# A hybrid FNet, retention and expert step: the Fourier branch over mirrored halves of channels and positions

## The reference

```python
h = _rmsnorm(x, norm1_g) * (1.0 + sc1) + sh1          # sc1, sh1, g1, ...: columns of silu(cond) @ w_ada
proj = h @ w_in                                       # 5120 columns: u_f 1024, q k v g 512 each, gate_f gate_r 1024 each
uf = u_f.reshape(b, length, 8, 128)
f_mix = jnp.fft.fftn(uf, axes=(1, 3), norm='ortho').real   # over positions and over the 128 channels of a group
f_out = f_mix.reshape(b, length, 1024) @ w_four
...                                                   # retention over q, k, v in both directions, group norm, silu(g)
merged = sigmoid(gate_f) * f_out + sigmoid(gate_r) * r_out
x = x + g1 * (merged @ w_o)
```

## Time and profile before

| | |
|---|---|
| Median of three runs | 971.39 us |
| Lowest and highest | 969.62 and 971.8 us |
| The profiled execution | 971.8 us |
| Its span, first to last instruction | 969.9 us |
| TensorE busy | 926.9 us, 96% |
| TensorE weight loads | 429.8 us, 44% |
| VectorE busy | 501.1 us, 52% |
| ScalarE busy | 211.4 us, 22% |
| Mean granted TensorE clock | 0.99 of full speed |

### The profile page before, as it was taken

The page is one execution under the profiler, slowest core; times in us unless marked ns, Lnnn a source line. Parts: engine busy times, 40 slices in busy tenths (PEclk is TensorE's granted clock), DMA queues, the critical chain, the costliest instruction groups (busy, mean ns, idle before and its releaser), DMA issues.

```text
span 969.9 us, 11638 instructions
## 1 busy us (share of the span) xinstructions
PE 926.9 (96%) x4219; PEld 429.8 (44%) x4251; DVE 501.1 (52%) x1045; ACT 211.4 (22%) x405; POOL 52.1 (5%) x68
## 2 busy tenths in 40 slices
PE   3999999999999999999999999999999999999992
PEld 2446444855555545853343333333333434333330
DVE  3102520695678673564454545454545454545457
ACT  4111201210000012512222222222222222222222
POOL 1010000100000000010000000000000000000000
PEclk9999999999999999999999999999999999999996
DMA  9993222304547646618999999999999999999901
GB/s 332 391 331 144 88 86 87 120 1 173 217 173 261 238 189 268 239 44 360 422 420 422 419 422 417 422 419 419 418 417 414 420 421 418 419 413 419 409 29 66
DMA packets 63995, 285.82 MB, mean 295 GB/s; under 512 B 6345, under 2 KB 6529, under 8 KB 38721
## 3 DMA queue, kind: packets, MB, share of 16 engines
q1 hardware_dynamic: 57216, 265.56, 68.6%
q0 software_dynamic: 6720, 19.50, 5.3%
HBM read 286.24 MB, written 3.80 MB: 299 GB/s over the span
## 4 chain that ended last, share of the span: by engine, by line
PE 92%; DMA 3%; DVE 2%; ACT 1%; issue 1%; SPq 0%; DVEq 0%; POOLq 0%; ACTq 0%
PE bank L1086 22%; PE bank L697 15%; PE bank L1119 13%; PE bank L1112 11%; PE bank L690 11%; PE bank L879 4%; DMA ring<-in_w_in 2%; PE bank L1022 2%; PE bank L920 2%; PE bank L713 2%; PE bank L1025 1%; PE bank L927 1%; PE bank L1097 1%; DMA VG<-h_rows,idx 1%; PE bank L965 1%; PE bank L745 1%
## 5 line engine op out<-in xcount | busy, mean ns | idle before, releaser
L1086 PE MATMUL bank<-ring,QK 128*64 128x512 f32 (+1 forms) x1184 | 225.3, 592 | 0.0
L1086 PEld LDWEIGHTS bank<-ring,QK 128*64 128x64 f32 (+1 forms) x1184 | 72.3, 130 | 147.7 <-issue 147.7
L1119 PE MATMUL bank<-Fm,VG 128*128 128x512 bf16 x544 | 124.5, 383 | 6.5 <-DVE Fm L1990 3.0
L1975 DVE TENSOR_TENSOR hT<-bank,hT 128x512 f32<-128x512 f32 x192 | 118.3, 683 | 5.3 <-PE bank L1119 4.2
L1112 PE MATMUL bank<-ring,VG 128*64 128x512 f32 (+1 forms) x592 | 116.9, 598 | 0.5 <-ACT VG L1433 0.5
L690 PE MATMUL bank<-ring,hT 128*128 128x512 f32 x240 | 103.8, 593 | 0.0
L1966 DVE SCALAR_TENSOR_TENSOR VG<-VG,cw,bank 128x256 f32<-128x256 f32 x32 | 15.4, 481 | 144.5 <-issue 138.1
L1984 DVE TENSOR_TENSOR Fm<-bank,Fm 128x512 f32<-128x512 f32 x64 | 44.3, 692 | 83.2 <-ACT Fm L1440 83.2
L1119 PEld LDWEIGHTS bank<-Fm,VG 128*128 128x128 bf16 x576 | 56.5, 99 | 67.9 <-DVE Fm L1990 3.7
L697 PE MATMUL bank<-hT,ring 128*128 128x384 f32 x256 | 85.4, 487 | 0.0
L1440 ACT CAST Fm<-bank 128x512 bf16<-128x512 f32 x64 | 37.5, 586 | 207.3 <-PE bank L1112 207.3
(11 more groups left out here) (367 smaller groups left out, 810.8 us busy)
## 6 DMA issues: line engine op xcount, KB each, us to landing
ring<-in_w_exp_gate SPq DMA_DIRECT2D x64, 1024.0 KB, 10.9
ring<-in_w_exp_up SPq DMA_DIRECT2D x64, 1024.0 KB, 13.2
ring<-in_w_exp_down SPq DMA_DIRECT2D x64, 1024.0 KB, 13.0
ring<-in_w_ada SPq DMA_DIRECT2D x12, 2048.0 KB, 10.8
ring<-in_w_in SPq DMA_DIRECT2D x10, 2048.0 KB, 16.9
ring<-in_w_four_out SPq DMA_DIRECT2D x2, 2048.0 KB, 7.7
ring<-in_w_out SPq DMA_DIRECT2D x2, 2048.0 KB, 11.2
ring<-in_w_ret_out SPq DMA_DIRECT2D x1, 2048.0 KB, 14.1
```

What stands on the lines that cost most here:

```text
L1086: ins = mm(ps[0][rows, :], xT[:, k, rows], expert(2 * s + n)[0][:, k, :, :], start=(k == 0), stop=(k == KC - 1))
L1119: ins = mm(ps[banks[g]][:, :], slotT[:, k, t * P:(t + 1) * P], y[:, h * 512:(h + 1) * 512], start=(n == 0), stop=(n == 2))
L1975: v.tensor_tensor(into, o, into, ALU.add).then_inc(sem("summed"), 1)
```

## The change

The position transform is linear over tokens and the projection over channels, so their order can be exchanged. Now x_hat itself is multiplied with the position tables (tiles pos0 to pos7), evicted by VectorE and ScalarE into `halves_T` and scaled there, and the projection to u runs over 194 columns of cosine and 194 of sine instead of 384 positions.

The channel transform of 128 real columns needs only sums of mirrored columns for its cosines and differences for its sines. VectorE therefore folds win0 and win1 in SBUF (`fold_odd`, `fold_even`): column c plus and minus column 128 - c, 256 columns a piece and a kind instead of 512. The unpaired middle column of each group goes apart (`middles`, tile um). The tiles uo0 to uo3 and ue0 to ue3 are the projections on both, 64 matmuls of 194 columns. Each tile ch0 to ch3 gets a sine matmul, a cosine matmul and four quarter ones for the middle columns; chm collects the middle outputs.

The rows of w_four_out are folded in the same manner: four0 loads rows 0 to 63 of each group in four transfers, four1 is a gather of the mirrored rows by GpSimd in four transfers after q2, four_mid has the middle rows. After the weighting of k, VectorE forms sums and differences in 16 steps of two operations. A Fourier output tile is then nine matmuls of 194 columns (`fourier`), and ScalarE copies its odd half out so that VectorE can form the 384 positions in four operations.

Beside this: the tables for positions move to the first constants piece (791 columns instead of 143), and VectorE's list starts with a wait for that piece and four index operations. win0 is loaded in two halves around ada3, and win1 before ada0. The transposes h1T move behind the shift sums, and their evictions apply scale and shift at once. The g1 sums and the row g1s move from the first loop to the end of the q, k, v, sw stage, their store with them. The order of slots changes, and six of the early expert transfers change their order.

```diff
+HG = P // 2
+CHUNK = 256
...
+    first = ["ident", "cols", "dft_lat", "dft_ctx"]
+    for k in first + [k for k in parts if k not in first]:
...
-PLACES = (("ada2", 0), ("ada3", 1), ("win0", 2), ("ada0", 3), ("ada1", 4), ("win1", 5), ("win2", 0), ("win3", 1), ("win4", 2),
-          ("win5", 3), ("win6", 4), ("four0", 5), ("ada4", 0), ("ada5", 1), ("win7", 2), ("four1", 3), ("ada8", 4), ("ada9", 5),
-          ("win8", 0), ("ret", 1), ("ada6", 2), ("ada7", 3), ("win9", 4), ("ada10", 5), ("out0", 0), ("ada11", 3), ("out1", 2))
+NFIRST = CONST_AT["dft_ctx"][1]
+
+
+PLACES = (("ada2", 0), ("win0", 2), ("ada3", 3), ("win1", 1), ("ada0", 4), ("ada1", 5), ("win2", 0), ("win3", 3), ("win5", 4),
+          ("win6", 5), ("win4", 2), ("four0", 1), ("four1", 0), ("ada4", 3), ("ada5", 2), ("win7", 4), ("ada8", 3), ("win8", 2),
+          ("ada9", 5), ("ret", 4), ("ada6", 0), ("ada7", 1), ("win9", 5), ("ada10", 3), ("ada11", 2), ("out0", 0), ("out1", 1))
...
-            "g1": (4, parts_a, MB[:, 0:512], bias),
+            "g1": (4, thirds(MB[:, :]) + thirds(work[:, :]), C[:, at:at + 512], bias),
...
+            n = j * D // CHUNK + at // CHUNK
+            home = four_spare if n == 0 else piece("four1")[:, (n - 1) * CHUNK:n * CHUNK]
...
+                if name == "win0":
+                    sp.dma_start(dst[:, 0:4, :], w_in[:, 0:4, 0:512]).then_inc(sem("win0_low"), 16)
...
+                elif name == "four0":
+                    dst = piece(name).rearrange("p (j n) -> p j n", j=4)
+                    for n in range(4):
+                        rows = w_four[n % 2:HG:2, n // 2:G:2, :]
+                        sp.dma_start(dst[n * 32:(n + 1) * 32, :, :], rows).then_inc(landed if n == 3 else sem("four0_low"), 16)
...
+                if name == "ada3":
+                    dst = piece("win0").rearrange("p (k n) -> p k n", k=KC)
+                    sp.dma_start(dst[:, 4:KC, :], w_in[:, 4:KC, 0:512]).then_inc(sem(f"piece_slot{PLACE['win0']}"), 16)
...
-            sp.wait_ge(sem("g2_weighed"), 4)
+            sp.wait_ge(sem("g2_weighed"), 2)
...
+            sp.wait_ge(sem("g2_weighed"), 4)
+            ahead(3, 1, w_eu, "gate_up_slot0")
+            ahead(3, 2, w_ed, "down_slot0")
...
+            computed(pool, "um")
+            pool.dma_start(four_mid, w_four[HG, :, :]).then_inc(sem("four_mid_in"), 16)
...
+            computed(pool, LAST_READ["win2"])
+            pool.wait_ge(sem("four_rows_ready"), 4)
+            for j in range(4):
+                stand_alone(pool, "pool_passed")
+                pool.indirect_dma_start(four_back(j, 0, D), None, A["w_four_out"].rearrange("o k n -> (o k) n"),
+                                        bass.IndirectOffsetOnAxis(idx[:, j:j + 1], 0), bounds_check=D - 1, oob_is_err=False).then_inc(sem("four1_in"), 16)
+            pool.wait_ge(sem("k_rotated"), 2)
+            load_bias("g1", 2)
+            store_row("g1")
...
+            def positions(k):
+                o = bank(f"pos{k}")
+                lat, ctx_part = const("dft_lat"), const("dft_ctx")
+                for c in range(2):
+                    mm(o[:, 0:2 * HL], x_hat[:, 1 + c, k * P:(k + 1) * P], lat[:, c * 2 * HL:(c + 1) * 2 * HL], start=(c == 0), stop=(c == 1))
+                done(mm(o[:, 2 * HL:2 * HALF], x_hat[:, 0, k * P:(k + 1) * P], ctx_part, start=True, stop=True))
...
+            def odd_channels(o, j, ks):
+                for k in ks:
+                    ins = mm(o[:, 0:HALF], odd_of[j // 2][k][:, j % 2 * P:(j % 2 + 1) * P], halves_T[:, k, HALF:2 * HALF], start=(k == 0), stop=(k == KC - 1))
+                return ins
+
+            def even_channels(o, j, ks):
+                for k in ks:
+                    ins = mm(o[:, 0:HALF], even_of(j // 2, k)[:, j % 2 * P:(j % 2 + 1) * P], halves_T[:, k, 0:HALF], start=(k == 0), stop=(k == KC - 1))
+                return ins
+
+            low, high = range(0, 4), range(4, KC)
+            pe.wait_ge(sem("x_normed_V"), 2)
+            pe.wait_ge(sem("x_normed_A"), 1)
+            for k in range(4):
+                positions(k)
+            pe.wait_ge(sem("cond_ready"), 2)
+            row_sums("sc1", 2, (0,))
+            positions(4)
+            positions(5)
+            row_turned("sc1", 0)
+            positions(6)
+            positions(7)
+            sc11, sc1t1 = bank("sc11"), bank("sc1t1")
+            uo = [bank("uo0"), bank("uo1")]
+            ue = [bank("ue0"), bank("ue1")]
+            for k in low:
+                pe.wait_ge(sem("scaled_A" if k % 2 else "scaled_V"), k // 2 + 1)
+            pe.wait_ge(sem("win_folded"), 1)
+            for j in range(2):
+                odd_channels(uo[j], j, low)
+            row_sums_in(sc11, "ada3")
+            pe.wait_ge(sem("win_folded"), 2)
+            even_channels(ue[0], 0, low)
+            row_turned_in(sc1t1, "sc1", 1)
+            even_channels(ue[1], 1, low)
+            for k in high:
+                pe.wait_ge(sem("scaled_A" if k % 2 else "scaled_V"), k // 2 + 1)
+            pe.wait_ge(sem("win_folded"), 3)
+            for j in range(2):
+                done(odd_channels(uo[j], j, high))
+            pe.wait_ge(sem("win_folded"), 4)
+            for j in range(2):
+                done(even_channels(ue[j], j, high))
+            pe.wait_ge(sem("win_folded"), 6)
+            for j in range(2, 4):
+                done(odd_channels(bank(f"uo{j}"), j, range(KC)))
             row_sums("sh1", 0)
+            pe.wait_ge(sem("win_folded"), 7)
+            done(even_channels(bank("ue2"), 2, range(KC)))
             row_turned("sh1", 0)
-            turn_and_project("sh1", "u02", 2)
+            done(even_channels(bank("ue3"), 3, range(KC)))
...
+            o = bank("um")
+            pe.wait_ge(sem("first_shifted"), 1)
             for k in range(KC):
-                q = k % 4 * 32
-                ins = mm(o[q:q + 32, :], shift_rep[:, k, :], win0.rearrange("p (k n) -> p k n", k=KC)[:, k, :], start=(k < 4), stop=(k >= KC - 4))
+                for i in range(2):
+                    q = (2 * i + k % 2) * 32
+                    middle = middles[:, i, k, :, :].rearrange("p r g -> p (r g)")
+                    ins = mm(o[q:q + 32, 0:HALF], middle, halves_T[:, k, 0:HALF], start=(k < 2), stop=(k >= KC - 2))
...
+            pe.wait_ge(sem("mean_shifted"), 2)
             for j in range(4):
-                positions(2 * j)
-                positions(2 * j + 1)
-                if j:
-                    channels(j - 1)
-
+                emptied(pe, f"uo{j}")
+                emptied(pe, f"ue{j}")
+                if j == 0:
+                    emptied(pe, "um")
+                o = bank(f"ch{j}")
+                mm(o[:, HALF:2 * HALF], const("chan_odd"), u_odd[j], start=True, stop=True)
+                mm(o[:, 0:HALF], const("chan_even"), u_even[j], start=True, stop=False)
+                for n in range(4):
+                    signs = const("mid_in")[:, 4 * j + n:4 * j + n + 1].broadcast_to([P, 32])
+                    ins = mm(o[n * 32:(n + 1) * 32, 0:HALF], signs, u_mid, start=False, stop=True)
+                done(ins)
+            o = bank("chm")
+            for j in range(4):
+                mm(o[0:32, 0:HALF], const("mid_out")[:, 6 - 2 * j:38 - 2 * j], u_even[j], start=(j == 0), stop=False)
+            done(mm(o[0:32, 0:HALF], const("mid_sum"), u_mid, start=False, stop=True))
...
+            def fourier(m):
+                o = bank(f"fo{m}")
+                for j in range(4):
+                    mm(o[:, HALF:2 * HALF], four_odd(j, m * P, P), mixed_odd[j], start=(j == 0), stop=(j == 3))
+                for j in range(4):
+                    mm(o[:, 0:HALF], four_even(j, m * P, P), mixed_even[j], start=(j == 0), stop=False)
+                done(mm(o[:, 0:HALF], four_mid[:, m * P:(m + 1) * P], mixed_mid[0:G, :], start=False, stop=True))
...
+                fourier(m)
...
+                    if kind == "gf":
+                        if m:
+                            emptied(act, f"fo{m - 1}")
+                        o = tile(f"fo{m}")
+                        nc.scalar.copy(odd_out, o[:, HALF:2 * HALF]).then_inc(sem("odd_out_ready"), 1)
...
+            v.memset(hTf[:, 0:12 * CHUNK:HG], 0.0)
+            v.memset(MB[:, 0:4 * CHUNK:HG], 0.0)
+            dve.wait_ge(sem("ident_in"), 16)
+            for j in range(4):
+                v.tensor_scalar(idx[:, j:j + 1], cols[:, 15:16], float(2 * P * j), None, ALU.add).then_inc(sem("four_rows_ready"), 1)
...
+            def fold_odd(i, lo, hi):
+                w = groups_of(i)[:, lo:hi, :, :]
+                for k in range(lo, hi):
+                    ins = v.tensor_copy(middles[:, i, k, :, :], groups_of(i)[:, k, :, HG].unsqueeze(1).broadcast_to([P, 8, 4]))
+                link(ins)
+                out = (MB[:, :] if i and lo else hTf[:, (8 * i + lo) * CHUNK:(8 * i + hi) * CHUNK]).rearrange("p (k g c) -> p k g c", g=4, c=HG)
```

(67 more changed lines are left out.)

366 lines of the change are left out of this document (164 added, 202 removed).

## The result

The changed kernel takes 940.87 us (median of 4 runs, 940.43 to 941.33), the kernel before 970.5 in the same comparison: a ratio of 0.970, 95% interval 0.968 to 0.971. The forecast was 937, with 929 to 951 as its range. The profiled execution has a span of 939.5 (run time 941.33), 4.2 more than the 935.3 of the sum.

What follows compares the result with a forecast made beforehand. TensorE, with 92% of the chain, was taken to bound the kernel. 74.0 + 82.4 + 16.8 + 2.0 + 130.7 + 629.4 = 935.3 of span, plus 1.9 minus 0.4 gave 936.8, say 937; range 929 to 951 (own range 931 to 943).

Steps and rivals of the forecast that it cites:

- Rival 1: Some 300 narrow passes on TensorE bound by the weight load, 0.19 us instead of 0.164: 7.8 us more, 945; chance 0.12.
- estimate of 944: The time if the Trainium skill's issue-gap rule added 25 ns to each of some 300 narrow TensorE passes.
- first gap: Opening: TensorE idles about 3.1 us while VectorE scales and folds the lower half of win0.
- clock loss: Opening: after TensorE's 3.1 us of idleness the clock is granted at half, costing 1.7 us.
- second gap: Opening: TensorE idles 2.1 us until VectorE has scaled and can fold the upper half at 41.2.
- the two terms (1.9 and 1.7): Opening on TensorE: 1.9 us for slow first transposes, kept from the trace, and 1.7 us for half clock after idleness.
- cover of 0.8 us: End of q, k, v, sw: VectorE's moved g1 sums end at 84.2, TensorE needs them for g1s at 85.0.
- each microsecond beyond is a stall of one: Before g1s: VectorE lateness past its 0.8 us of slack stalls TensorE one for one; 0 was booked.
- Eight outputs of 9 x 0.328 = 2.95: First gate and output loop: each Fourier output tile priced as nine 194-column matmuls of 0.328 us, 2.95 a tile.
- such seams: Second gate and output loop: 0.6 us booked beside the gates, outputs and two rows of 0.99.
- rival 3: The four1 gather lands late for VectorE's fold: in series +10 us, 947, chance 0.06; slower still, some 975, 0.03.
- rival 4: The change doesn't halve the work: TensorE keeps 384 columns, time 971 to 985; chance 0.02.

Runs made afterwards that it cites:

- the run with 4.3 us more: Changed kernel with six additions of 512 elements put on VectorE between the fold of the output weights and the g1 sums: 948.18 us, ratio 0.977.

## Why the prediction was right

**Mechanism and size.** TensorE bounds both kernels, and the time fell with its work. 31.9 us of busy time went instead of 35.5; the loops' 2.9 and the channels' 0.7 below are about the difference. The stages' gains are read from the chain; no run takes the opening's 16.3 us apart into the order of transforms and the folded channels.

**Narrow passes.** The line through the other widths held: 32 passes of 194 columns,

```profile
46.36 5.25 PE bank L762 x32
```

are 0.164 each. Rival 1 (0.19, the weight load's length) is refuted, although a load does take 190 ns. With it goes the estimate of 944. By the Trainium skill, "TensorE: Matmul & The Clock Gate", section "Back-to-back issue gap", narrow matmuls in a stream with weight loads are spaced wider than their columns ask. This f32 trace does not show that at 194 columns: 0.164 us, for the 0.162 that the forecast gave to the columns.

**Opening**, 74.0 forecast, 74.61 measured. The constants landed at 9.4 and not 9.9, TensorE began at 13.13 and not 13.8; the fold was ready at 29.06 and not 29.8; first gap 2.92 (3.1), clock loss 1.67 (1.7), second gap 2.16 (2.1), no loss. The clock loss behind the gap came as forecast in this profile and not in four others, so that it came here was luck; in three of these four the start was cold for longer, so the sum of the two terms (1.9 and 1.7) was steadier than either. Against these small gains stands the channel tile. In the chain its two full matmuls take 0.33 each in the first tile, but 0.52 and 0.33 in the three tiles that follow a quarter matmul, and the four quarter ones take 0.47 for 0.43. The tiles are 1.13 and three times 1.32, 5.1 for the 4.4 forecast: the 0.7 that the stage lost. It is again a full matmul behind a partial one, here partial in its output rows (32 of 128) and not in the rows that it sums over.

**q to g1s**: 101.57 for 101.2. The cover of 0.8 us was 0.9. That it held so closely is in part luck, since it is the difference of two sums of some 85 us each. The forecast booked "each microsecond beyond is a stall of one"; the run with 4.3 us more shows that this line was too cheap: 8.0.

**Loops**, the step that failed in size. "Eight outputs of 9 x 0.328 = 2.95" took the ninth matmul, of 8 rows, at the price of a 128-row one. It is 3.14, and the gate behind it 5.36 for 5.16. Eight times 0.19 and seven times 0.20 are 2.9. The row that should have warned was in the trace before: behind the quarter matmuls of a row, 32 passes of 384 columns take 10.52 us, 0.20 more than 32 x 0.3225. The forecast booked 0.6 for such seams in the second loop and none in the first, where the ninth matmul makes one in every tile. It was priced by its columns only.

**Loads.** The gathered four1 was in time; its four transfers were issued 1.3 us apart and overlapped. ret was in time. Median from issue to landing in us, last number:

```profile
ring<-in_w_ret_out SPq DMA_DIRECT2D x1, 2048.0 KB, 7.8
ring<-in_w_four_out,idx POOLq DMA_INDIRECT x4, 5.1
```

So rival 3 didn't come. Nor did rival 4: an output tile's two sets of four matmuls run over 194 columns each and take 1.31 a set.

**Rest**: 629.7 for 629.4. In sum 0.6 + 0.4 + 2.9 + 0.3 = 4.2 us of span above the forecast.

## What to carry to other kernels

Price a matmul by its columns and also by whether its shape, in rows summed over and in output rows, is that of its neighbours: a remainder of 8 rows in a stream of full ones was 0.39 us a tile cheaper when padded with zeros to 128. A helper engine that is late can cost more than its lateness, since the clock may fall behind the wait (3.6 us of waiting became 8.0 here); put VectorE work where TensorE is busy for long, and count how much cover is left. When a change removes TensorE work from a loop, look for what else stands in that loop: here half of the matmuls without the moved sums gave 12.7 of 20.6 us.

## What the runs showed of the hardware that was not expected

- An f32 matmul of 194 columns over 8 or 64 rows, between matmuls over 128 rows, takes 0.52 instead of 0.328, and what follows 0.20 more. At both seams the weight load of 0.19 starts with its matmul and not ahead of it. Over 128 rows, mostly zeros, both extras are gone.
- Among the shorter gaps the length didn't decide the clock. Behind the first gap, 2.91 or 2.92 us in six profiles, it fell to 0.50 in two and stayed at 1.00 in four. Behind the second, 2.16 or 2.17 in nine, it fell once. Gaps of 3.59 and 3.69 were both followed by 0.50, as was the one of 3.41 in the kernel before; the first two cost about as much again as they lasted. What else decides stays open. In the seven gaps that were filled with matmuls the clock stayed, two of them of the kind that falls once in nine: too few to call it shown.
- TensorE's cold start varied between executions of the same code: in the five kernels with the change's own opening, the second position group took 1.39 to 1.93 and the third 1.04 to 1.65. The granted clock reads 1.00 through it. The two with the shortest cold start (1.39 and 1.58, then 1.04) are the two that lost the clock behind the first gap. With ten passes of filling ahead of them the groups took 1.14 and 1.04, or 1.36 and 1.04.
